# Start and end cut into smaller pieces, the recurrent layer reordered, and its decay square moved from GpSimd to ScalarE

## The reference

```python
def rglru_mixer(h, ...):
    u = h @ w_in
    xb, gate = u[..., :D_RNN], u[..., D_RNN:]
    xb = causal_depthwise_conv(xb, conv_w, conv_b)
    xblk = xb.reshape(bsz, s, 16, 96)
    r = sigmoid(einsum('bsnc,ncd->bsnd', xblk, w_a) + b_a)
    i = sigmoid(einsum('bsnc,ncd->bsnd', xblk, w_x) + b_x)
    log_a = -8 * r * softplus(-lam)
    a = exp(log_a)
    bt = sqrt(-expm1(2 * log_a)) * (i * xb)
    _, hseq = associative_scan(_lin_rec_combine, (a, bt))
    return (hseq * silu(gate)) @ w_out
...
o = mixer(rms_norm(x, norm_pre)); x = x + rms_norm(o, norm_post)
```

## Time and profile before

| | |
|---|---|
| time, median of 3 runs | 2327.02 us (2326.95 to 2328.91) |
| the profiled execution's own time | 2325.19 us |
| its span | 2323.4 us |
| mean granted TensorE clock | 0.987 |
| PE busy | 2228.3 us (96%) |
| DVE, ACT, POOL busy | 1223.7, 805.9, 535.4 us |

### The profile page before, as it was taken

The page is one execution under the profiler, slowest core; times in us unless marked ns, Lnnn a source line. Parts: engine busy times, 40 slices in busy tenths (PEclk is TensorE's granted clock), DMA queues, the critical chain, the costliest instruction groups (busy, mean ns, idle before and its releaser), DMA issues.

```text
span 2323.4 us, 26702 instructions
## 1 busy us (share of the span) xinstructions
PE 2228.3 (96%) x10598; PEld 1789.9 (77%) x10598; DVE 1223.7 (53%) x1986; ACT 805.9 (35%) x1344; POOL 535.4 (23%) x347
## 2 busy tenths in 40 slices
PE   7999999998999999999999999999888979999997
PEld 6878886887788888876667888888776857877876
DVE  4665556465654443355457444433879675443343
ACT  3334333434232232233443323222467323323321
POOL 2442334250511011113324011022045131110100
PEclk9999999999899999999999999999999999999999
DMA  4222222221223333332222333333222322222321
GB/s 143 82 64 82 82 73 64 64 73 64 71 93 100 93 98 100 93 103 87 74 64 82 100 93 98 100 93 98 91 77 87 92 76 73 95 72 79 94 73 73
DMA packets 84155, 198.27 MB, mean 85 GB/s; under 512 B 7216, under 2 KB 44208, under 8 KB 84032
## 3 DMA queue, kind: packets, MB, share of 16 engines
q1 hardware_dynamic: 81408, 189.62, 26.4%
q10 hardware_dynamic: 2624, 6.93, 0.9%
HBM read 194.40 MB, written 2.13 MB: 85 GB/s over the span
## 4 chain that ended last, share of the span: by engine, by line
PE 85%; DVE 8%; ACT 3%; issue 2%; POOL 1%; DMA 1%; DVEq 0%; SPq 0%; POOLq 0%; ACTq 0%
PE PS L541 49%; PE PS L585 5%; PE PS L587 5%; PE PS L586 5%; PE PS L610 2%; PE PS L611 2%; PE PS L612 2%; PE PS L1060 2%; PE PS L658 1%; PE PS L668 1%; PE PS L682 1%; DVE WL L1660 1%; PE PS L913 1%; PE PS L903 1%; ACT WH L1095 1%
## 5 line engine op out<-in xcount | busy, mean ns | idle before, releaser
L1660 DVE TENSOR_TENSOR WL<-WR,WH 128x1024 fp32r<-128x1024 f32 x353 | 484.2, 1378 | 729.0 <-ACT WH L1095 728.6
L1095 ACT ACTIVATE WH<-WR 128x1024 fp32r<-128x1024 f32 x353 | 370.4, 1055 | 694.0 <-DMA WR<-in_ws 682.5
L541 PE MATMUL PS<-XH,WH 128*128 128x512 f32 x1024 | 403.9, 394 | 19.0 <-ACT XH L1104 11.8
L541 PE MATMUL PS<-XL,WH 128*128 128x512 f32 x1024 | 400.1, 391 | 0.0
L541 PE MATMUL PS<-XH,WL 128*128 128x512 f32 x1024 | 400.0, 391 | 0.0
L541 PEld LDWEIGHTS PS<-XH,WH 128*128 128x128 f32 x1024 | 193.3, 189 | 63.7 <-issue 13.4
L585 PE MATMUL PS<-XH,WH 128*128 128x512 f32 x544 | 224.1, 412 | 4.8 <-DVE WL L1660 3.6
L541 PEld LDWEIGHTS PS<-XL,WH 128*128 128x128 f32 x1024 | 193.4, 189 | 41.2 <-issue 1.4
L541 PEld LDWEIGHTS PS<-XH,WL 128*128 128x128 f32 x1024 | 193.2, 189 | 40.8
L587 PE MATMUL PS<-XH,WL 128*128 128x512 f32 x544 | 215.2, 396 | 0.0
L586 PE MATMUL PS<-XL,WH 128*128 128x512 f32 x544 | 214.1, 394 | 0.0
(11 more groups left out here) (320 smaller groups left out, 3754.3 us busy)
## 6 DMA issues: line engine op xcount, KB each, us to landing
WR<-in_ws SPq DMA_DIRECT2D x281, 512.0 KB, 3.6
WR<-in_ws SPq DMA_DIRECT2D x144, 256.0 KB, 3.2
B_CB<-gates ACTq DMA_DIRECT2D x8, 512.0 KB, 4.0
XTOK<-in_x SPq DMA_DIRECT2D x2, 1024.0 KB, 8.4
out<-OUT SPq DMA_DIRECT2D x4, 512.0 KB, 2.6
R_D<-in_decay ACTq DMA_DIRECT2D x4, 256.0 KB, 2.6
GAIN<-in_post ACTq DMA_DIRECT2D x1, 512.0 KB, 4.8
CST<-in_cst SPq DMA_DIRECT2D x1, 320.0 KB, 3.4
```

The source lines that it names most:

```text
L541: mm = pe.matmul(PS[:, bank + o, :], l, r, start=first and kk == 0 and i == 0, stop=last and kk == 1 and i == 2)
L1095: nc.scalar.activation(WH[:, s, :], WR[:, s, :], ACT.Copy).then_inc(hi_ready, 1)
L1660: tt(WL[:, s, :], WR[:, s, :], WH[:, s, :].bitcast(F32), ALU.subtract).then_inc(lo_ready, 1)
```

## The change

It has three parts. **Beginning:** x comes in four quarters of 512 KB (`x_part`); only the identity part of `CST` is loaded ahead of it, the first quarter stands before the first weight unit and the other three behind it, and the rest of `CST` comes with the fourth unit (`rest_in`). The two tables `A_COS` and `A_SIN` are loaded later. PE turns four tiles, does the first half of unit 0, turns the other four and goes on; the turned tiles use six PSUM banks. ACT loads its function table by a small instruction ahead of the data, and takes over from DVE the copies into `R`.

**Recurrent layer:** POOL's square goes to ACT as an activation (`decay_squares`); the order of sigmoids, splits, `decays`, `out_sigmoids`, `softplus`, `out_inputs` and `outputs_lows` is another.

**End:** of the last eight units four are multiplied as before, the last four token block by token block, so that one PSUM bank after the other is complete (`fin_done`). Squares, factor, scaling and output run by token block, with eight transfers of 256 KB.

```diff
@@ block.sync
-            sp.dma_start(CST[:, :], cst).then_inc(consts_in, 16)
-            for i in range(2):
-                columns = slice(T * i, T * i + T)
+            def quarter(i):
+                columns = slice(256 * i, 256 * i + 256)
                 sp.dma_start(XTOK[:, :, columns], x...[:, :, columns])
-                    .then_inc(x_half[i], 16)
+                    .then_inc(x_part[i], 16)
+            sp.dma_start(CST[:, IDENT:IDENT + P], ...).then_inc(consts_in, 16)
+            quarter(0)
             for u in range(UNITS):
+                if u == 1:
+                    for i in range(1, 4):
+                        quarter(i)
+                if u == 3:
+                    sp.dma_start(CST[:, ONES:NCST], ...).then_inc(rest_in, 16)
...
@@ block.tensor, beginning
+            def turn_x(ks):
+                for k in ks:
+                    if k % 2 == 0:
+                        pe.wait_ge(x_part[k // 2], 16)
+                    if k >= 6:
+                        pe.wait_ge(r_done, k - 5)
+                    for b in range(TB):
+                        mm = pe.transpose(PS[:, 2 + k % 6, ...], XTOK[...], ident)
+                    mm.then_inc(x_turned, 1)
+            turn_x(range(4))
...
                     next(body)
+                    if m == 0 and i == 0:
+                        turn_x(range(4, DT))
...
@@ block.tensor, end
-            group(U["RO"] + 8, 8, YH, YL, 4, stationary=False)
+            for j in range(4):
+                unit(U["RO"] + 8 + j, j, YH, YL, 4, j == 0, False, False)
+            for b in range(TB):
+                for j in range(4, 8):
...
+                mm.then_inc(fin_done, 1)
@@ block.scalar, beginning
+            nc.scalar.activation(RB[:, T:T + 4], VC[:, 0:4], ACT.Copy).then_inc(act_warm, 1)
+            x_high(range(1))
+            split(1)
+            x_high(range(1, 2))
+            x_kept(range(2))
+            x_high(range(2, 6))
+            split(2)
+            x_high(range(6, 8))
             split(3)
+            x_kept(range(2, 8))
@@ block.scalar, recurrent layer
+            def decay_squares(j):
+                act.wait_ge(ae_done, 6 * j + 3)
+                act.wait_ge(ix_done, j + 1)
+                nc.scalar.activation(L_W[...3 tiles], L_A[j % 2], ACT.Square).then_inc(e_done, 1)
...
             split(u + 21)
+            gate_sigmoids(1)
+            split(u + 22)
             out_sigmoids(0)
-            split(u + 22)
-            gate_sigmoids(1)
             split(u + 24)
             decays(1)
+            decay_squares(1)
             split(u + 25)
             energy_root(1)
             split(u + 26)
             gate_sigmoids(2)
             split(u + 28)
             decays(2)
+            recurrent_high(0)
+            decay_squares(2)
             split(u + 29)
-            recurrent_high(0)
+            gate_sigmoids(3)
             out_sigmoids(1)
-            split(u + 30)
-            gate_sigmoids(3)
             split(u + 31)
             energy_root(2)
             decays(3)
+            decay_squares(3)
             split(u + 32)
@@ block.gpsimd
-                pool.wait_ge(ix_done, j + 1)
-                pool.wait_ge(ae_done, 6 * j + 3)
-                nc.gpsimd.tensor_tensor(L_W[:, tiles, :], L_A[i], L_A[i], ALU.mult).then_inc(e_done, 1)
@@ block.vector, recurrent layer
             energy(0)
             split(u + 20)
+            out_inputs(0)
             recur(0)
-            split(u + 21)
-            out_inputs(0)
+            split(u + 22)
             split(u + 24)
...
             split(u + 28)
+            outputs_lows(0)
             out_inputs(1)
             split(u + 29)
-            outputs_lows(0)
             energy(2)
...
             split(u + 32)
+            energy(3)
             outputs_lows(1)
-            energy(3)
@@ block.vector, end (for each token block b)
+                tt(total, ...); ts(total, ...); scaled_out(4 + b)
+                dve.wait_ge(fin_std, b + 1)
+                nc.vector.reciprocal(...)
+                (two output tiles)
```

More of the change, by code:

```diff
@@ L215, in program @@
             sem("sel_in"))
-        x_half = [sem(f"x_half{i}") for i in range(2)]
-        x_turned = sem("x_turned")
+        x_part = [sem(f"x_part{i}") for i in range(4)]
+        x_turned, act_warm, rest_in = sem("x_turned"), sem("act_warm"), sem("rest_in")
         r_done = sem("r_done")
@@ L513, in _ @@
             for tb in range(TB):
-                sp.wait_ge(o_ready, 2 * tb + 2)
-                sp.dma_start(out[tb * P:(tb + 1) * P, :], OUT[:, tb, :]).then_inc(out_done, 16)
-            sp.wait_ge(out_done, 16 * TB)
+                for d in range(2):
+                    w = slice(T * d, T * d + T)
+                    sp.wait_ge(o_ready, 2 * tb + d + 1)
+                    sp.dma_start(out[tb * P:(tb + 1) * P, w], OUT[:, tb, w]).then_inc(out_done, 16)
+            sp.wait_ge(out_done, 32 * TB)
         @block.tensor
@@ L1082, in _ @@
             pe.wait_ge(rt_ready, 4)
-            group(U["RO"] + 8, 8, YH, YL, 4, stationary=False)
+            for j in range(4):
+                unit(U["RO"] + 8 + j, j, YH, YL, 4, j == 0, False, False)
+            for b in range(TB):
+                for j in range(4, 8):
+                    u = U["RO"] + 8 + j
+                    if b == 0:
+                        pe.wait_ge(lo_ready, u + 1)
+                    for kk in range(2):
+                        yh, yl = (y[:, 2 * j + kk, b * P:(b + 1) * P] for y in (YH, YL))
+                        wh, wl = (w[:, u % RING, kk * T:(kk + 1) * T] for w in (WH, WL))
+                        pe.matmul(PS[:, 4 + b, :], yh, wh, start=False, stop=False)
+                        pe.matmul(PS[:, 4 + b, :], yh, wl, start=False, stop=False)
+                        mm = pe.matmul(PS[:, 4 + b, :], yl, wh, start=False, stop=j == 7 and kk == 1)
+                mm.then_inc(fin_done, 1)
         @block.scalar
@@ L1146, in attend, with x_high, x_kept @@
                     nc.scalar.activation(A_YH[:, t, :], A_Y[:, t, :], ACT.Copy).then_inc(x_hi, 1)
-            for d in range(2):
-                for k in range(4 * d, 4 * d + 4):
+            def x_high(ks):
+                for k in ks:
                     act.wait_ge(x_turned, k + 1)
-                    nc.scalar.activation(XH[:, k, :], PS[:, k, :], ACT.Copy,
+                    nc.scalar.activation(XH[:, k, :], PS[:, 2 + k % 6, :], ACT.Copy,
                                          scale=VC[:, VEC["a_norm"] + k:VEC["a_norm"] + k + 1]).then_inc(x_hi, 1)
-                    if k == 1:
-                        split(1)
+            def x_kept(ks):
+                for k in ks:
+                    act.wait_ge(x_lo, k + 1)
+                    nc.scalar.activation(R[:, k, :], PS[:, 2 + k % 6, :], ACT.Copy).then_inc(r_done, 1)
+            x_high(range(1))
[5 more added lines that the diff above has]
+            x_high(range(6, 8))
             split(3)
+            x_kept(range(2, 8))
+            act.dma_start(A_COS[:, :], turn_a[0]).then_inc(rota_in, 16)
+            act.dma_start(A_SIN[:, :], turn_a[1]).then_inc(rota_in, 16)
             for k in range(DT):
+                if k == 4:
+                    split(4)
                 act.wait_ge(r_done, k + 1)
@@ L1322, in conv_high, with gate_sigmoids @@
                 nc.scalar.activation(CH[:, c, :], L_XC[:, c % 4, :], ACT.Copy).then_inc(ch_ready, 1)
-            def gate_sigmoids(j):
+            def gate_sigmoids(j, first=0, last=6):
                 for which, (dst, bias) in enumerate(((L_R[j % 2], "b_a"), (L_I[j % 2], "b_x"))):
@@ L1328, in gate_sigmoids @@
                         q = 3 * which + o
+                        if not first <= q < last:
+                            continue
                         if o == 2:
@@ L1373, in _ @@
             u = U["L"]
-            for j in range(3):
+            for j in range(2):
                 for o in range(4):
                     last_tap(4 * j + o)
-                if j == 2:
-                    split(u + 18)
-                    gate_sigmoids(0)
                 for o in range(4):
-                    split(u + min(4 * j + 9 + o, 18))
+                    split(u + 4 * j + 9 + o)
                     conv_high(4 * j + o)
-                    if j == 2 and o == 1:
-                        decays(0)
+            split(u + 17)
+            last_tap(8)
+            gate_sigmoids(0, 0, 2)
+            last_tap(9)
+            gate_sigmoids(0, 2, 3)
+            last_tap(10)
+            gate_sigmoids(0, 3, 4)
+            last_tap(11)
+            split(u + 18)
+            conv_high(8)
+            gate_sigmoids(0, 4, 6)
+            conv_high(9)
+            decays(0)
+            conv_high(10)
+            conv_high(11)
+            decay_squares(0)
             split(u + 19)
```

91 lines of the change are left out of this document (46 added, 45 removed).

## The result

| | before | after |
|---|---|---|
| median of the runs (lowest to highest), us | 2326.98 (2326.87 to 2328.91) | 2311.98 (2308.77 to 2312.69) |
| profiled execution: time, span, us | 2325.19, 2323.4 | 2312.69, 2310.9 |
| ratio of the times, 95% interval | | 0.9931 (0.9914 to 0.9948) |

The kernel is 15 us faster by the medians, 12.5 us by the two profiled executions. The forecast was 2307.5 with 2300 to 2313. The whole falls inside, near its upper end and 1 us above the forecast's own range of 2303 to 2311; the terms in it are to be read one by one.

A forecast was written before the change was run, and what follows sets the result against it. PE was taken to bound the kernel, 85% of the span, leaving its idle time and the ends to win. 10.1 + 6.4 + 2.8 = 19.3 us from 2325.19 gave 2305.9, 2307.7 as median; stated 2307.5, range 2300 to 2313.

The forecast's parts named there:

- The beginning: Kernel start: first product at 9.4 instead of 15.96, five units done at 39.6 instead of 49.77; 10.1 us won.
- The end: After the last matmuls: last output tile at 2313.9 instead of 2320.3; 6.4 us won (6.1 to 6.8).
- The layer: Recurrent layer, summed body by body: 2.8 us won, with two long waits of 6 and 9 us left.
- Body 0: Recurrent layer's first body: the wait shrinks from 6.8 to 1.2 and its clock loss goes; 7.1 us won.
- nothing for one under 2 us: Clock-loss rule for PE's waits: 1.7 us charged for each above about 4 us, none for one under 2 us.
- unit 20: Recurrent layer: its low part, behind `recur(0)`, comes at 1717.3 where PE wants it at 1715.6; 1.8 us lost.
- body 2: Recurrent layer: gates 2's sigmoid comes late, a wait of 6 us with 1.7 of clock; balance from 11.8 to 5.3.
- Body 3: Recurrent layer: unit 30's low part comes at 1787.0, a 9 us wait at low clock; balance 2.1 left.
- The exclusion of VectorE and GpSimd: Recurrent layer: a DVE instruction with two SBUF operands and a POOL instruction exclude each other and take turns.
- The case without it: Rival that the recurrent layer wins more (14 in 100): without the exclusion it gives 11 us, 2299.
- Wins nothing: Rival: the recurrent layer wins nothing or loses a few us, 2310 to 2314; 10 in 100.
- The slower one: Rival: ACT's square waits for POOL's product, holding the next unit; decides from 7 us a body, 2335; 2 in 100.

The follow-up runs named there:

- the filling products: The changed kernel plus nine products of a zeroed tile ahead of the first transposes and four between them: 2307.13 us, ratio 0.9915.
- the end alone: The kernel before with only the change's end, beginning and layer as before: 2321.17 us, ratio 0.9977.
- the layer alone: The kernel before with only the change's recurrent layer, beginning and end as before: 2326.93 us, ratio 0.9998.

## Why the prediction was right, and where its terms were off

The number, 2311.98, is inside the stated range of 2300 to 2313 because that range had been made to take in most of the case that the layer gives nothing, and this is the case that came. The two ends carried the gain, as forecast. The layer was forecast 2.8 us too high and the beginning 1.4 to 4 us too high by the traces, the end at most 0.8 too low. That the whole is right is in part luck.

- **The beginning**, 10.1 forecast, 8.65 at the statistics row against the profile of before. The transfers streamed: the second quarter was there at 8.58 and the first product at 10.20, 0.8 late. The step that failed is the half unit counted at 2.7 us. At the lower clock the nine products up to 14.15 took 3.95 us, 1.9 more than at full pitch; the filling products show that this is the clock. I had seen the clock column at 1.00 there in the profile of before and counted no start at the lower level. The 16 transposes were 1.3 us cheaper than counted (1.66 between starts instead of 3.0). Sum: 0.8 + 1.9 - 1.3 = 1.4 us less. A second thing was off in the term: it counts from 49.77, the latest of the three statistics rows of this beginning, so the slow stretch behind 25.30 was counted as always there. Against the other two the beginning is worth 6.1 and 7.5 us, by the medians 6.7.
- **The way to the layer**, counted at nothing, and rightly. The 3.0 us lost in the profiles compared are the lucky execution of before. The sum had added its luck back at the end (2305.9 to 2307.7), but only the 1.8 us by which it was under its median.
- **The end**, 6.4 forecast, 7.2 by the trace, 5.8 (3.3 to 7.4) by the medians of the end alone. Right, with 3.2 us from the last matmul to the last tile where 3.4 was said. The 0.8 us more in the trace are mostly the way from the last tile to the end of the span: 2.4 us instead of 3.1, where 0.3 less was allowed for.
- **The layer**, 2.8 forecast; -0.3 by the trace and nothing by the layer alone. The mechanism was right: the wait of body 1 went, and the two long ones came where they were named and by whom (8.16 us where 6 was said, 9.36 where 9). Three terms were mis-sized. Body 0 won 4.7 us in place of 7.1, since unit 16 landed 4.6 us after its slot was free and not 3.7, and the wait of 2.11 us that was left cost clock as well; "nothing for one under 2 us" was too simple. And unit 20 was not waited for (1.8 us had been charged): its low part ended at 1712.07 and PE, later by the 2.4 us that body 0 had not won, wanted it at 1712.38. So after body 1 the balance was 11.2 us, near the 11.8 forecast, by two misses that cancel. Then body 2 took 8.6 us of it in place of 6.5: gates 1 ended 2.4 us later than counted, and the chain to the sigmoids with them, while PE came to body 2 only 0.6 later. Body 3 took 3.0 in place of 2.5.
- **The square on ScalarE** was priced at 1.2 to 3.6 us and took 1.48. Back on GpSimd it costs some 3 us of time, the most of it at unit 30.
- **The exclusion of VectorE and GpSimd**, which the sum rested on: shown by the same instruction beside GpSimd and alone (product 4.97 and 1.75, scans 6.55 and 3.45, low part 4.50 and 1.2). The case without it, 2299, did not come. The Trainium skill (VectorE: DVE Perf Modes, Two Vector instructions with no wait between them) says that a Vector instruction with two SBUF inputs reads one of them through an interface shared with GpSimd; these rows agree, and give its price.
- **The rivals.** "Wins nothing" (10 in 100, 2310 to 2314) is what came, in the layer and in the time. The slower one's mechanism exists (5 us, in body 3) but was hidden behind a longer chain, and far from its 7 us a body.

## What to carry to other kernels

When a wait ends with a long chain over three engines, look in each queue for the work that stands ahead of the chain's next link and is not wanted yet: one swapped pair on GpSimd was worth 7 us, where moving a square from GpSimd to ScalarE was worth some 3. When such an edit only removes a wait at one weight unit, the next unit's part is often behind the same queue, so follow it until PE meets no wait. Fill TensorE's idle time at the start with products whose result is overwritten; here that brought the first milestone 2.5 us forward. And before a difference of a few us between two profiles is explained, look at the same stretch in a profile where nothing was changed: here the reference profile itself was 3 us off.

## What the runs showed of the hardware

- Whether the clock falls after a short wait differs from run to run of the same place. In the layer, waits of 1.78, 1.82, 2.11 and 2.53 us had a stretch at the lower level behind them (PE at 1.2 of its 2.4 GHz, clock 0.72 over the next 6 us, 1.7 us lost), and waits of 1.62, 1.63, 2.09 and 2.50 us had none (1.00). Those of 3.96 us and more always had one there. At 25.30 a wait of 3.60 us had none in one execution (1.00) and one in another (0.67), with the same instructions.
- The Trainium skill (TensorE: Matmul & The Clock Gate, What's actually happening) says that the same kernel is measured with different numbers of cold products, those at the lower clock at its start. The traces agree: with the new beginning and no filling products, four to nine of the first products are slow, at 0.43 us or in part so.
- The clock falls without a wait as well: no later than 1 us behind the 24 statistics products with one output column, which run from 41.98 to 46.7 in the changed kernel, products of full length came to run at 0.43 us in every kernel here.
- Between 10 and 15 us the clock column says 1.00 in the changed kernel, for products at 0.43 us: there the pitch of the products has to be read, not the column.
- A VectorE instruction with two inputs in SBUF and a GpSimd instruction hold each other up: unit 20's low part, 1.2 us alone, began 0.28 us behind GpSimd's sum (3.59 us, to 1712.94), took 4.50 us and so ended 1.2 us behind it.
